# One subtraction of the decayed score blocks: from a GpSimd instruction into a per-head bias of ScalarE's clamp

## The reference, cut to what matters

```
a_cum = jnp.cumsum(dtg * A.reshape(g, e), axis=2)
seg = a_cum[:, :, :, None] - a_cum[:, :, None, :]          # a_i - a_j
decay = jnp.exp(jnp.where(causal, seg, -jnp.inf))
cb = jnp.einsum('bcign,bcjgn->bcijg', Cg, Bg)
y_diag = jnp.einsum('bcijg,bcijge,bcjgep->bcigep', cb, decay, xdt)
```

## Time and profile before

| | |
|---|---|
| median of three runs | 1153.3 us (1152.9 to 1154.33) |
| the profiled execution | 1155.78 us |
| its span, first to last instruction | 1154.0 us |
| busy: TensorE / VectorE / ScalarE / GpSimd | 1056.6 / 623.5 / 450.9 / 366.9 us |
| chain that ended last | TensorE 69%, VectorE 14%, ScalarE 4%, GpSimd 1% |

### The profile page before, as it was taken

How to read it: one execution, slowest core, us unless ns; L and a number is a source line. 1 busy time by engine, 2 the same in 40 slices (tenths; PEclk the granted TensorE clock), 3 DMA queues, 4 the chain that set the end, 5 groups by cost and what they waited for, 6 DMA issues and landing times.

```text
span 1154.0 us, 18893 instructions
## 1 busy us (share of the span) xinstructions
PE 1056.6 (92%) x7588; PEld 977.5 (85%) x7588; DVE 623.5 (54%) x1450; ACT 450.9 (39%) x784; POOL 366.9 (32%) x274
## 2 busy tenths in 40 slices
PE   6979999999999999978889998899988999889978
PEld 4879799979998999858878888888888988879868
DVE  3112632254225421548694678757787577875682
ACT  3322552246135612462334452234522435225252
POOL 2131132313331233115340544405434064440340
PEclk9989999999999999989998898998989989896889
DMA  6441222221222122111325423154231552315303
GB/s 195 141 157 51 92 74 76 60 92 42 87 79 92 37 74 80 55 37 37 95 77 150 138 86 119 39 149 151 72 119 38 149 154 70 119 38 154 115 11 87
DMA packets 143144, 106.37 MB, mean 92 GB/s; under 512 B 10259, under 2 KB 133317, under 8 KB 142865
## 3 DMA queue, kind: packets, MB, share of 16 engines
q1 hardware_dynamic: 116408, 92.37, 25.9%
q10 hardware_dynamic: 26648, 12.80, 4.2%
HBM read 92.42 MB, written 16.79 MB: 95 GB/s over the span
## 4 chain that ended last, share of the span: by engine, by line
PE 69%; DVE 14%; ACT 4%; issue 4%; DMA 4%; SPq 3%; POOL 1%; ACTq 0%; DVEq 0%; POOLq 0%
PE pp L976 17%; PE pp L978 16%; PE pp L977 16%; PE pT_ L1196 3%; DMA w_raw_buf<-in_w_attn_in 2%; DVE cv L1625 2%; PE pS L1050 2%; DVE cv L1604 2%; PE pO L1214 1%; PE pT_ L1246 1%; DVE cv L1602 1%; PE pO L1260 1%; SPq L424 1%; PE pO L1025 1%; PE pS L1187 1%
## 5 line engine op out<-in xcount | busy, mean ns | idle before, releaser
L538 POOL TENSOR_TENSOR w_lo_buf<-w_raw_buf,w_hi_buf 128x512 fp32r<-128x512 f32 x226 | 306.2, 1386 | 620.5 <-ACT w_hi_buf L602 549.7
L976 PE MATMUL pp<-h_hi,w_hi_buf 128*128 128x280 f32 x1296 | 404.7, 312 | 28.1 <-DVE rb L1578 19.6
L977 PE MATMUL pp<-h_lo,w_hi_buf 128*128 128x280 f32 x1296 | 386.3, 298 | 0.0
L978 PE MATMUL pp<-h_hi,w_lo_buf 128*128 128x280 f32 x1296 | 386.2, 298 | 0.0
L976 PEld LDWEIGHTS pp<-h_hi,w_hi_buf 128*128 128x128 f32 x1296 | 254.4, 196 | 40.1 <-issue 18.1
L977 PEld LDWEIGHTS pp<-h_lo,w_hi_buf 128*128 128x128 f32 x1296 | 254.2, 196 | 4.9 <-issue 4.3
L978 PEld LDWEIGHTS pp<-h_hi,w_lo_buf 128*128 128x128 f32 x1296 | 253.4, 195 | 0.0
L602 ACT ACTIVATE w_hi_buf<-w_raw_buf 128x2048 fp32r<-128x2048 f32 (+1 forms) x57 | 107.2, 1889 | 25.5 <-DMA w_raw_buf<-in_w_attn_in 12.6
L1419 DVE TENSOR_TENSOR x<-x,pp 128x280 f32<-128x280 f32 x128 | 56.6, 445 | 98.5 <-PE pp L978 98.1
L976 PE MATMUL pp<-og_hi,w_hi_buf 128*128 128x280 f32 x256 | 76.3, 298 | 5.1 <-DVE og_lo L1524 4.6
L976 PE MATMUL pp<-y_hi,w_hi_buf 128*128 128x280 f32 x256 | 76.5, 299 | 2.1 <-DVE x L1419 1.2
(11 more groups left out here) (280 smaller groups left out, 1750.7 us busy)
## 6 DMA issues: line engine op xcount, KB each, us to landing
w_raw_buf<-in_w_attn_in SPq DMA_DIRECT2D x16, 1024.0 KB, 5.1
w_raw_buf<-in_w_ssm_in SPq DMA_DIRECT2D x16, 1024.0 KB, 5.9
w_raw_buf<-in_w_attn_out SPq DMA_DIRECT2D x8, 1024.0 KB, 5.5
s_in<-in_state_ssm SPq DMA_DIRECT2D x32, 256.0 KB, 4.4
out<-s_in SPq DMA_DIRECT2D x32, 256.0 KB, 3.1
seg<-a_scratch ACTq DMA_DIRECT2D x16, 512.0 KB, 4.1
w_raw_buf<-in_w_ssm_out SPq DMA_DIRECT2D x8, 1024.0 KB, 5.5
w_raw_buf<-in_w_attn_in SPq DMA_DIRECT2D x8, 512.0 KB, 6.1
```

The lines of the kernel that those rows point to most:

```text
L538: ins = pool.tensor_tensor(w_lo_buf[n % LO_SLOTS][:, piece], raw[n % RAW_SLOTS][:, piece], w_hi_buf[n % HI_SLOTS][:, piece].bitcast(F32), ...
L976: pe.matmul(dst, hi[:, k, cols], a_hi[:, k, tk], start=(k == 0), stop=False)
L977: pe.matmul(dst, hi[:, k, cols], a_lo[:, k, tk], start=False, stop=False)
L978: mm = pe.matmul(dst, lo[:, k, cols], a_hi[:, k, tk], start=False, stop=(k == depth - 1))
```

## The change

GpSimd's subtraction goes, with its semaphore and its two waits. ScalarE waits for the DMA itself. The clamp takes a_j as its bias: Relu(-e + a_j). A bias is one number per partition, and a_j differs from head to head, so the clamp becomes eight instructions of 128 columns (of 32 in u=0). The exp stays one instruction.

```diff
                     if u == (2 if g + 1 < GROUPS else 5):
                         split_lo(slab_no[("z", s, 1)] + 2)
 
-                    if u != 1:
-                        pool.wait_ge(dt_tok, 3)
-                        pool.wait_ge(*seg_landed(g, u))
-                        e = seg[seg_no(u) % 2][0:n, :, 0:n]
-                        a_j = tok2[0:n, 1, c, SSM_H * g:SSM_H * (g + 1)].unsqueeze(2).to_broadcast([n, SSM_H, n])
-                        pool.tensor_tensor(e, e, a_j, ALU.subtract).then_inc(seg_done, 1)
                     decay_state(g, u - 1)
...
                 def decays(u):
-                    w = 5 * g + seg_no(u)
-                    n = LEN[ORDER[u]]
-                    act.wait_ge(seg_done, w + 1)
+                    w, c = 5 * g + seg_no(u), ORDER[u]
+                    n = LEN[c]
+                    act.wait_ge(dt_tok, 3)
+                    act.wait_ge(*seg_landed(g, u))
                     e = seg[seg_no(u) % 2][0:n, :, 0:n]
 
-                    act.activation(e, e, ACT.Relu, scale=-1.0).then_inc(clamped, 1)
+                    for h in range(SSM_H):
+                        ins = act.activation(e[:, h, :], e[:, h, :], ACT.Relu, scale=-1.0,
+                                             bias=tok2[0:n, 1, c, SSM_H * g + h:SSM_H * g + h + 1])
+                    ins.then_inc(clamped, 1)
                     act.wait_ge(clamped, w + 1)
                     act.activation(e, e, ACT.Exp, scale=-1.0).then_inc(l_done, 1)
```

More of the change, by code:

```diff
@@ L320, in build @@
         sx_ready = sem("sx_ready")
-        seg_done, l_done, m_done = sem("seg_done"), sem("l_done"), sem("m_done")
+        l_done, m_done = sem("l_done"), sem("m_done")
         a_done, xw_done, b_done = sem("a_done"), sem("xw_done"), sem("b_done")
@@ L565, in _ @@
                 split_lo(slab_no[("z", s, 1)] + 1)
-                for u, c in enumerate(ORDER):
-                    n = LEN[c]
+                for u in range(UNITS):
                     if u == (2 if g + 1 < GROUPS else 5):
                         split_lo(slab_no[("z", s, 1)] + 2)
-                    if u != 1:
-                        pool.wait_ge(dt_tok, 3)
-                        pool.wait_ge(*seg_landed(g, u))
-                        e = seg[seg_no(u) % 2][0:n, :, 0:n]
-                        a_j = tok2[0:n, 1, c, SSM_H * g:SSM_H * (g + 1)].unsqueeze(2).to_broadcast([n, SSM_H, n])
-                        pool.tensor_tensor(e, e, a_j, ALU.subtract).then_inc(seg_done, 1)
                     decay_state(g, u - 1)
```

## The result

The changed kernel takes 1159.3 us in the median (1158.95 to 1159.87, 4 runs), against 1153.8 for the kernel before, run beside it (1152.9 to 1155.29, 4 runs): ratio 1.0047, interval 1.0029 to 1.0064, so 5.5 us slower. The forecast was +2.8 us and 1156.1, with a range up to 1159.2. The sign was right, the size half of what came, and the time lies just above the range.

The account below looks back on a forecast made before the run. TensorE, busy 92%, was taken as the bound, its five waits at L1246 and anything newly late deciding the time. 3 x 0.34 + 1.0 + 0.82 gave +2.8 us; forecast median 1156.1 (+0.25%), range 1153.4 to 1159.2.

Parts of the forecast that it names:

- The trains: ScalarE's eight clamps: 2.45 us for 128 rows, 1.80 for 32 rows (u=0), each +1.39 us over one clamp.
- L1730's successor: VectorE's d_done instruction of unit 2: without L576 at the port, 0.69 us instead of 1.28.
- no clamp of u=4 or 5 waits for its transfer: The seg DMA wait, moved to ScalarE, costs 0 at u=4 and u=5; a transfer 2.5 us longer would begin to cost.
- the multiplication of u=4: VectorE's L1693: arrives about 0.1 us before GpSimd's third split piece, ends at 808.5 against 808.64 in group 1.
- The wait at u=4: TensorE's wait for the decayed product at L1246, in each of four groups: still about 1.3 us.
- The new wait for sT: TensorE at L1196 of group 3, behind the later sT copies: a new wait of 1.0 us or a little more.
- Rival 1: Multiplication of u=4 misses the port: +1.05 us per group; all four 5.6 us, 1158.9; chance 0.32 (all 0.15).
- Rival 2: Clamp train hardly longer than one clamp (under 1.3 us): u=4 waits vanish, -6 us, 1147; chance 0.04.
- the squares: Gate and squares behind u=5: 0.8 us later, TensorE waits at the sum; 0.34 us in each of groups 0 to 2.
- the 0.15 of u=4: Multiplication of u=4 ends sooner, so TensorE gains 0.15 us there; counted inside the 0.34 per group.
- 0.82 us, ahead of the serial tail: u=5 in group 3, where TensorE already waits for the product: the clamp's delay goes in whole, 0.82 us.

Follow-up runs that it names:

- e6: Changed kernel with the clamps and exp of u=0 moved two sT copies later; 1159.3 us, ratio 1.0041 to the kernel before.
- e8: Kernel before, with only the clamp of u=5 in group 3 made eight instructions, without a bias; 1155.6 us, ratio 1.0004.
- e1: Changed kernel with one clamp instruction per block, the first head's a_j as bias for all eight heads; 1150.2 us, ratio 0.9969.
- e3: Changed kernel with GpSimd's last state decay of each group (L551 of u=5) waiting for VectorE's first gated part of y; 1157.6 us, ratio 1.0026.
- the repeat: Changed kernel again, unedited, beside the runs of another batch; 1159.5 us, ratio 1.0046 to the kernel before.
- e9: Changed kernel with load_ec(4) and load_ec(5) behind their unit's clamp and exp in ScalarE's queue, groups 0 to 2 only; 1152.8 us, ratio 0.9981.
- e2: Kernel before, subtraction kept on GpSimd, with the clamp as eight biased instructions (a_j taken off twice); 1171.6 us, ratio 1.0151.
- e4: Changed kernel with load_ec(4) and load_ec(5) behind their unit's clamp and exp in ScalarE's queue, exp of ec a step later; 1150.3 us, ratio 0.9965.
- e7: Changed kernel with both the queue order of e4 and the late u=0 clamps of e6; 1150.0 us, ratio 0.996.
- e10: Changed kernel with the queue order of e4 in group 3 alone; 1156.5 us, ratio 1.0015.
- e5: Kernel before, subtraction still on GpSimd, with the queue order of e4; 1156.9 us, ratio 1.0017.

## Why the forecast was half right

**Right, by the step.** The trains take 2.45 and 1.80 us, GpSimd is busy 330 us and ScalarE 478 (forecast 332 and 479), L1730's successor takes 0.69, no clamp of u=4 or 5 waits for its transfer, and the multiplication of u=4 wins the port: it starts at 805.26, 0.16 us ahead of the end of GpSimd's second piece, and runs its 1.24 us unhindered. The wait at u=4 is 1.25 (forecast about 1.3), that at u=5 of group 3 is 3.00 (2.8). The new wait for sT is 0.54 and 0.36, about half of the 1.0 forecast, and removing it (e6) changed the time by nothing that can be told; e8, with the clamp of u=0 as it was before, shows such a wait too (1.4 us). Rival 1 named almost the time that came (1158.9), but its mechanism, a missed port at u=4, is in neither profile of the changed kernel: those waits would read 2.4 us; that it named the time is luck. Rival 2's condition, a short clamp, is what e1 sets up (1.16 us): it gained 3.9 us where the rival had 6; the wait at u=4 stayed in group 3 (1.2 us).

**The first term that was mis-sized: the squares.** I wrote 0.34 us for each of groups 0 to 2, which is 0.49 for the squares less the 0.15 of u=4. The stretches show 1.25, 1.26 and 0.75 us (group 2 had a wait of its own in the kernel before) where 0.49 stood. By e3, of 1.26 some 0.79 is the first square's lateness, which is what the 0.49 stood for: the squares start 2.96 us behind the u=5 product (818.71 - 815.75) against 1.97 before, 0.99 later where the forecast had 0.95 (0.8 and the 0.15 of u=4), so TensorE is late by 0.67, and the restart behind the wait takes 0.1 more. The other 0.47 is a collision I had not looked for: the gate, moved by about 1 us, meets L551 of u=5 at the port that VectorE and GpSimd share. I had followed the port lock at u=4, where the change removes an instruction, and not at the gate, where it only moves one. Together +1.8 us beyond the forecast (3.26 against 3 x 0.49). The lock that the Trainium skill's page "SBUF — State Buffer" (SBUF: two separate sides) states agrees with both places: the gate's 2.88 us beside L551, and GpSimd's third split piece, 2.25 us instead of about 1.28 beside the multiplication of u=4.

**The second: "0.82 us, ahead of the serial tail".** The wait grew by 1.02, and the stretch behind it by 1.55 in one profile of the changed kernel and 1.00 in the other (20.81 and 20.26 against 19.26). I priced a wait at its length alone and took the stretch behind it for unchanged. What the rows show in its place is TensorE's clock. In the first profile all of the 3.8 us behind the wait ran at 0.50, and VectorE's next state update starts 6.9 us behind the product instead of 5.9. In the repeat it starts at 5.7, and the loss comes later, as in e8: the clock is back about 20.2 us behind the product, not 17.7.

The sum from these: 3.26 for the squares, about -0.65 for u=4 in four groups, 1.02 for the last wait, 1.0 to 1.55 for the stretch behind it, 0.36 to 0.54 for sT: 5.0 to 5.7 us. The medians differ by 5.5 and, in the repeat, 4.8. The fit is partly luck, since the sum leaves out what stands under "Open".

**Open.** The cause of the longer end isn't shown. In six profiles with a wait of 2.6 to 3.0 us (the changed kernel twice, e3, e6, e8, e9) the product took 1.97 or 1.98 us, in five with 1.3 to 1.9 (e1, e2, e4, e7, e10) 1.09 us; but e5 took 1.59 us behind 3.70, and e2 1.09 behind 2.47. The length of the wait alone doesn't order them.

From the end of group 2 to the product of u=2 in group 3, work that is the same but for u=0, the two profiles of the changed kernel take 103.3 and 103.4 us against 101.8 before, at a granted clock of 0.83 against 0.85. Only the wait for sT in it is in the sum. In e3 the same stretch took 101.1 at 0.90, with a wait for sT of 2.5 us in it, in e8 100.8; in e4 it took 103.7. So it moves with the clock by up to 3 us, and whether the change has a part in it isn't known. The two first profiles also differ by 2.8 us before the first group's blocks begin, in favour of the changed kernel, in work that the change doesn't touch; the repeat's profile stands 1.3 us behind the changed kernel's at the same place, which is why I used the lengths of stretches and not starts.

All prices against the kernel before rest on one profile of it, and e8's groups 0 and 1 show that the same code can take 0.8 to 0.9 us more there.

## What to carry to other kernels

Before moving work off an engine that a profile shows others waiting for, look at what the receiving engine's queue holds ahead of that work: here a DMA issue that waits for a third engine bounded the clamp. Four runs show the parts: the move with the train of clamps in the old order loses 5.5 us, the new order without the move loses 2.2 (e5), both together gain 3.9 to 4.8 (e4, e7), and the move with one clamp gains 3.9 in the old order (e1). So the move paid as soon as either the train or the place of the issue was out of the way. When an edit delays a chain, follow it to the next place where it meets another engine at a shared port, not only to the next wait. Split an instruction into parts only with the price of a part in hand: seven more parts cost 1.39 us, five times a group.

## What the runs showed of the hardware

A per-partition operand has a price on ScalarE: the eight clamps of 128x128 without a bias took 1.71 us, 297 ns each alone (e8), with a bias 2.45 us and 387 ns. In both, neighbours overlap by 92 to 95 ns ((8 x 387 - 2450) / 7 = 92, (8 x 297 - 1710) / 7 = 95).

The port lock works in both directions. Beside the multiplication of u=4, GpSimd's third split piece took 2.25 us instead of about 1.28.

The clock often falls at or behind an idle stretch of TensorE, but not by its length alone: 1.34 us of waiting left it at 1.00 (e10), 1.98 us brought 0.60 over the next 3.2 us, 3.00 us brought 0.50 over the next 3.8 (both at the end of group 3), while in e2 the product behind 2.47 us ran at full clock. What it costs can lie far behind: in e8 the 1.2 us are lost 18 us after the wait.
